# A second feed-forward product made of seven block products instead of eight, in two sweeps over its weights

## The reference, cut to what matters

```python
def hybrid_layer(x, ...):
    ...
    h = rms_norm_2(x, norm_mlp)
    return x + jnp.square(jax.nn.relu(h @ w_ff1)) @ w_ff2     # w_ff1 [1024, 4096], w_ff2 [4096, 1024]

def second_block(x, ...):
    ...
    return rms_norm_2(x, norm_final)
```

## Time and profile before

| what | value |
|---|---|
| median of three runs | 1082.27 us (1082.26 to 1082.41) |
| the profiled execution's own time | 1083.03 us |
| its span, first to last instruction | 1081.2 us |
| TensorE busy | 1060.9 us, 98% |
| VectorE / ScalarE / GpSimd busy | 555.6 / 477.5 / 125.7 us |

### The profile page before, as it was taken

One profiled execution on the slowest core, in us unless ns is written; L12 is line 12 of the kernel. 1 busy time (PEld: TensorE's weight loads), 2 busy tenths in 40 slices (PEclk: granted clock), 3 DMA queues, 4 the chain that ended last, 5 costly groups with the idle time before them and its releaser, 6 DMA issues.

```text
span 1081.2 us, 14121 instructions
## 1 busy us (share of the span) xinstructions
PE 1060.9 (98%) x5460; PEld 869.6 (80%) x5460; DVE 555.6 (51%) x1096; ACT 477.5 (44%) x893; POOL 125.7 (12%) x158
## 2 busy tenths in 40 slices
PE   9999999999899999999999999999999999999997
PEld 7788878888788888978777778898888888888885
DVE  5578997666874235434577777442222213333334
ACT  8454345555542433344677843233344433222223
POOL 0022110003400005400434400000000000000000
PEclk9999999999999999999999999999999999999999
DMA  8554333124220573132100642044222322233002
GB/s 320 113 125 99 98 93 80 43 59 158 88 88 1 157 243 115 39 81 76 40 2 1 215 156 98 1 160 171 78 78 81 140 91 78 78 96 138 1 1 79
DMA packets 74802, 104.28 MB, mean 96 GB/s; under 512 B 3904, under 2 KB 41536, under 8 KB 74736
## 3 DMA queue, kind: packets, MB, share of 16 engines
q1 hardware_dynamic: 73808, 100.60, 28.8%
q0 software_dynamic: 784, 2.75, 1.7%
q10 hardware_dynamic: 144, 0.03, 0.0%
HBM read 98.52 MB, written 4.85 MB: 96 GB/s over the span
## 4 chain that ended last, share of the span: by engine, by line
PE 84%; DVE 8%; ACT 3%; DMA 3%; issue 1%; SPq 1%; POOL 0%; DVEq 0%; ACTq 0%
PE bank L759 70%; PE bank L916 3%; PE bank L1092 2%; PE bank L897 2%; PE bank L906 2%; DVE x L1778 1%; PE bank L1014 1%; DVE stats L1777 1%; DMA arena<-in_x 1%; PE bank L1101 1%; DMA wring<-in_w_in 1%; PE bank L1115 1%; DVE u_lo L1682 1%; PE bank L807 1%; DVE x L2147 0%
## 5 line engine op out<-in xcount | busy, mean ns | idle before, releaser
L2119 DVE TENSOR_TENSOR w_lo<-wring,w_hi 128x1024 fp32r<-128x1024 f32 x64 | 78.4, 1225 | 238.1 <-ACT w_hi L1597 238.1
L1597 ACT ACTIVATE w_hi<-wring 128x1024 fp32r<-128x1024 f32 x64 | 67.7, 1058 | 211.4 <-PE bank L759 211.4
L759 PE MATMUL bank<-u_hi,h_hi 128*128 128x512 f32 (+1 forms) x288 | 111.0, 385 | 1.5 <-ACT arena L1240 1.0
L759 PE MATMUL bank<-u_hi,h_lo 128*128 128x512 f32 (+1 forms) x288 | 109.1, 379 | 0.0
L759 PE MATMUL bank<-u_lo,h_hi 128*128 128x512 f32 (+1 forms) x288 | 109.0, 379 | 0.0
L1682 DVE TENSOR_TENSOR u_lo<-wring,u_hi 128x1024 fp32r<-128x1024 f32 (+1 forms) x64 | 78.9, 1241 | 53.5 <-ACT u_hi L1332 53.0
L759 PE MATMUL bank<-h_hi,w_lo 128*128 128x512 f32 (+2 forms) x272 | 104.5, 384 | 0.0
L1332 ACT ACTIVATE u_hi<-wring 128x1024 fp32r<-128x1024 f32 (+1 forms) x64 | 65.9, 1034 | 87.3 <-PE bank L759 62.8
L759 PE MATMUL bank<-h_hi,w_hi 128*128 128x512 f32 (+2 forms) x272 | 104.4, 384 | 0.0
L759 PE MATMUL bank<-h_lo,w_hi 128*128 128x512 f32 (+2 forms) x272 | 104.3, 384 | 0.0
L759 PE MATMUL bank<-w_lo,ff_hi 128*128 128x512 f32 x256 | 101.1, 395 | 0.0
(11 more groups left out here) (296 smaller groups left out, 2065.3 us busy)
## 6 DMA issues: line engine op xcount, KB each, us to landing
wring<-in_w_ff SPq DMA_DIRECT2D x16, 2048.0 KB, 8.1
wring<-in_w_in SPq DMA_DIRECT2D x60, 512.0 KB, 3.9
arena<-in_w_out SPq DMA_DIRECT2D x4, 1024.0 KB, 5.0
wring<-in_w_out SPq DMA_DIRECT2D x2, 2048.0 KB, 12.6
arena<-in_first SPq DMA_DIRECT2D x8, 418.0 KB, 6.1
arena<-in_x SPq DMA_DIRECT2D x4, 512.0 KB, 10.7
arena<-bias_copies POOLq DMA_DIRECT2D x8, 256.0 KB, 6.4
arena<-bias_copies SPq DMA_DIRECT2D x32, 64.0 KB, 2.2
```

Of the source, the lines that this page charges most:

```text
L759: last = mm(b, lhs, rhs, start=(start and n == 0), stop=(stop and n == 2))
L1597: run(dst, src, ACT.Copy).then_inc(w_hi_done, 1)
L2119: v.tensor_tensor(cut(w_lo[ring3(m)]), src, cut(w_hi[ring3(m)]).bitcast(F32), ALU.subtract).then_inc(w_lo_done, 1)
```

## The change

The hidden channels are taken in 16 pairs of 128-channel chunks, a and b. The tokens are cut into two halves of 256, the output columns into two halves of 512. With two chunks, two token halves and two output halves a pair has eight block products; here seven are made, of sums and differences of blocks, and added into the output blocks with signs. In a first sweep over all pairs four products are made (24 matmuls of the same shape per pair: 4 products by 2 token tiles by 3), in a second sweep three (18 matmuls per pair). So 16 x 42 = 672 matmuls stand where 768 did. `w_ff2` is read from HBM twice, a pair (1 MB) at a time, into six places.

The block sums are made in place by GpSimd: `side_totals` on `ffT` (two of 128x256 per pair, while the first product runs), `side_sum` (128x256 per pair of the first sweep), `weight_sums` (one of 128x1024 and one of 128x512 per pair in the first sweep, two of 128x512 in the second). VectorE makes one further difference (`side_diff_done`, 512 columns) per pair of the first sweep. Highs and lows are made for whole pairs: the weights' 2048 columns in the first sweep and 1536 in the second, the tokens' side 256 + 768 and 256 + 512. The rings for the highs are four pairs deep (`place_free`, on `pair_used`).

Between the sweeps the last two pairs of the first are run bank by bank, and VectorE adds eight banks into `x` in twelve adds; the last four pairs (`held`) of the second sweep are also run bank by bank. The final norm's order is rewritten; for two of the four token tiles ScalarE scales and GpSimd multiplies by the gain.

The core of the diff:

```diff
+PAIR = 2 * D
+PAIR_PLACES = 6
+NP = NF // 2
+HELD = 4
 ...
@@ sync
+            for m in range(2 * NP):
+                if m < PAIR_PLACES:
+                    sp.wait_ge(w_lo_done, 4 * (6 + m // 2))
+                else:
+                    sp.wait_ge(pair_used, m - PAIR_PLACES + 1)
+                rows = w["w_ff2_2"][2 * P * (m % NP):2 * P * (m % NP + 1), :]
+                sp.dma_start(pair_raw(m).rearrange("p (k n) -> p k n", k=2), rows.rearrange("(k p) n -> p k n", p=P))\
+                    .then_inc(piece_in[pair_place(m)], 16)
@@ tensor
-            for k in range(NF - 2):
 ...
+            def product(m, t, b, tokens, cols, start, stop, low=0):
+                w = (s_hi[m % 4], s_lo[pair_place(m)])
+                f = (f_hi[m % 4], f_lo[m % 4])
+                token = slice(tokens + t * P, tokens + (t + 1) * P)
+                high, lows = slice(cols, cols + S), slice(low + cols, low + cols + S)
+                mm(b, f[0][:, token], w[0][:, high], start=start, stop=False)
+                mm(b, f[1][:, token], w[0][:, high], start=False, stop=False)
+                return mm(b, f[0][:, token], w[1][:, lows], start=False, stop=stop)
+            for m in range(NP - 2):
+                pe.wait_ge(f_lo_done, m + 1)
+                for q in range(4):
 ...
+                    for t in range(2):
+                        last = first_of(m, q, t)
+                last.then_inc(pair_used, 1)
+            for q in range(4):
+                for t in range(2):
+                    for m in (NP - 2, NP - 1):
+                        pe.wait_ge(f_lo_done, m + 1)
+                        last = first_of(m, q, t)
 ...
+            for m in range(NP, 2 * NP - HELD):
+                pe.wait_ge(f_lo_done, m + 1)
+                for q in range(3):
+                    for t in range(2):
 ...
+                        last = second_of(m, q, t)
@@ scalar
+            def place_free(m, side):
+                if m >= 4:
+                    act.wait_ge(pair_used, m - 3)
 ...
+            def pair_high(m):
+                place_free(m, "w")
+                act.wait_ge(w_summed, 2 * m + 2)
+                at = 0 if m < NP else S
+                run(s_hi[m % 4][:, 0:PAIR - at], pair_raw(m)[:, at:PAIR], ACT.Copy).then_inc(s_hi_done, 1)
@@ vector
+            def lows(m):
+                f, hi, lo, total = ff_pair(m % NP), f_hi[m % 4], f_lo[m % 4], f_sum[m % 4]
+                if m < NP:
+                    dve.wait_ge(side_sum_done, m + 1)
+                    by = total[:, 256:512].unsqueeze(1).to_broadcast([P, 2, 256])
+                    v.tensor_tensor(total[:, 512:D].rearrange("p (q s) -> p q s", q=2), f[:, 256:768].rearrange("p (q s) -> p q s", q=2),
+                                    by, ALU.subtract).then_inc(side_diff_done, 1)
+                at = 0 if m < NP else S
+                dve.wait_ge(s_hi_done, m + 1)
+                v.tensor_tensor(s_lo[pair_place(m)][:, at:PAIR], pair_raw(m)[:, at:PAIR], s_hi[m % 4][:, 0:PAIR - at].bitcast(F32), ALU.subtract)
+                dve.wait_ge(f_hi_done, m + 1)
 ...
+            for m in range(NP + 2):
+                lows(m)
 ...
+            for m in range(NP + 2, 2 * NP):
+                lows(m)
@@ gpsimd
+            def side_totals(j):
+                pool.wait_ge(a_free, AT[("ff", 2 * j + 1)] + 1)
+                f = ff_pair(j)
+                g.tensor_tensor(f[:, 256:512], f[:, 256:512], f[:, 768:D], ALU.add)
+                g.tensor_tensor(f[:, 512:768], f[:, 512:768], f[:, 0:256], ALU.add)
+            def side_sum(m):
+                if m >= 4:
+                    pool.wait_ge(pair_used, m - 3)
 ...
+                g.tensor_tensor(f_sum[m % 4][:, 256:512], f[:, 0:256], f[:, 768:D], ALU.add).then_inc(side_sum_done, 1)
+            def weight_sums(m):
+                pool.wait_ge(piece_in[pair_place(m)], 16 * (m // PAIR_PLACES + 2))
+                raw = pair_raw(m).rearrange("p (q n) -> p q n", q=4)
+                if m < NP:
+                    g.tensor_tensor(raw[:, 1:3, :], raw[:, 1:3, :], raw[:, 0:4:3, :], ALU.add).then_inc(w_summed, 1)
+                    pool.wait_ge(w_summed, 2 * m + 1)
+                    g.tensor_tensor(raw[:, 3, :], raw[:, 3, :], raw[:, 0, :], ALU.add).then_inc(w_summed, 1)
+                else:
+                    g.tensor_tensor(raw[:, 1, :], raw[:, 1, :], raw[:, 3, :], ALU.subtract).then_inc(w_summed, 1)
+                    g.tensor_tensor(raw[:, 2, :], raw[:, 2, :], raw[:, 0, :], ALU.subtract).then_inc(w_summed, 1)
+            for j in range(NP - 1):
+                side_totals(j)
 ...
+            weight_sums(2)
+            side_totals(NP - 1)
+            side_sum(1)
+            weight_sums(3)
+            side_sum(2)
+            for m in range(4, 2 * NP):
+                weight_sums(m)
+                if m <= NP:
+                    side_sum(m - 1)
```

More of the change, by code:

```diff
@@ L1171, in _ @@
             R += 2 * NT
-            NF = DFF // P
             def ff_tile(c, first, end):
@@ new lines, in _ @@
+            held = range(2 * NP - HELD, 2 * NP)
+            for m in held[:-1]:
+                pe.wait_ge(f_lo_done, m + 1)
+                for t in range(2):
+                    second_of(m, 0, t)
+            pe.wait_ge(f_lo_done, 2 * NP)
+            for t in range(2):
+                second_of(2 * NP - 1, 0, t).then_inc(p_full, 1)
+            for q in (1, 2):
+                for t in range(2):
+                    for m in held:
+                        last = second_of(m, q, t)
+                    last.then_inc(p_full, 1)
@@ L1625, in _ @@
[L1625 to L1632, removed]
+                if c == NF - 3:
+                    pair_high(0)
+                    side_high(0)
@@ new lines, in _, with square @@
+                if c == NF - 2:
+                    pair_high(1)
+            side_high(1)
+            for m in range(2, 2 * NP):
+                pair_high(m)
+                side_high(m)
+            def square(order, i, n, seen):
+                act.wait_ge(added, seen)
+                if order >= 2:
+                    act.wait_ge(ss_done, 3 * NT + order - 1)
+                run(junk[:, 512 * (order % 2):512 * (order % 2 + 1)], x[:, i, 512 * n:512 * (n + 1)], ACT.Square, accum_out=ssf[:, 2 * i + n:2 * i + n + 1])\
+                    .then_inc(ss_done, 1)
@@ L2149, in _ @@
-            dve.wait_ge(gfin_in, 16)
[L2150 to L2156, removed]
-                        finish(i - 1)
-                    if n == 0:
-                        dve.wait_ge(ss_done, 3 * NT + 2 * i + 1)
-                        v.tensor_scalar(first_half[:, i:i + 1], ssf[:, 2 * i:2 * i + 1], 1.0 / D, EPS, ALU.mult, ALU.add).then_inc(half_done, 1)
@@ new lines, in finish @@
+            def finish(n, i):
+                dve.wait_ge(inverse_done, n + 1)
+                for c in (slice(0, 512), slice(512, D)):
+                    v.scalar_tensor_tensor(x[:, i, c], x[:, i, c], rsf[:, i:i + 1], gfin[:, c], ALU.mult, ALU.mult).then_inc(y_done, 1)
+            for m in range(NP + 2):
+                lows(m)
+            for t in range(2):
+                dve.wait_ge(p_full, 1 + t)
+                add(2 + t, t, 0, ALU.add)
+                add(2 + t, 2 + t, 1, ALU.add)
@@ new lines, in _ @@
+            for t in range(2):
+                dve.wait_ge(p_full, 3 + t)
+                add(4 + t, 2 + t, 1, ALU.subtract, 2 * t + 2)
+                add(4 + t, 2 + t, 0, ALU.add)
+            for t in range(2):
+                dve.wait_ge(p_full, 5 + t)
+                add(6 + t, 2 + t, 1, ALU.add, 2 * t + 5)
+            for t in range(2):
+                dve.wait_ge(p_full, 7 + t)
+                add(t, t, 0, ALU.add, 2 * t + 1)
+            for m in range(NP + 2, 2 * NP):
+                lows(m)
@@ new lines, in _ @@
+            dve.wait_ge(gfin_in, 16)
+            for t in range(2):
+                dve.wait_ge(p_full, 9 + t)
+                add(2 + t, 2 + t, 1, ALU.add, 9 + t)
+                add(2 + t, t, 1, ALU.add)
+            half_of(2, 1, 1)
+            half_of(3, 1, 2)
+            dve.wait_ge(p_full, 11)
+            add(4, 2, 0, ALU.add, 6)
+            add(4, 0, 0, ALU.add, 11)
+            invert(0, 2)
+            finish(0, 2)
+            dve.wait_ge(p_full, 12)
+            add(5, 3, 0, ALU.add, 8)
```

200 lines of the change are left out of this document (126 added, 74 removed).

## The result

Three executions of the changed kernel took 1111.04, 1114.19 and 1115.25 us against 1082.26 us before: the ratio is 1.0289, 95% interval 1.0264 to 1.0315, slower. (A fourth execution took 5842 us; it is left out of the ratio, and nothing here explains it.) The profiled execution took 1115.25 us, its span is 1113.4 us, 32.2 more than before.

The account below looks back on a forecast made before the run. The matmul count bounds the second product before; after, alternating VectorE and GpSimd turns do. Steps reach E + 210.1 against E + 178.0, so +32.1 us with an unchanged tail: span 1113.3, time 1114 us, range 1095 to 1137.

Parts of the forecast that it names:

- What is removed: Second product: 768 - 672 = 96 matmuls at 0.2316 us go, 22.2 us, the whole gain if other engines keep pace.
- Rival (a): Second product: VectorE and GpSimd overlap after all, leaving stalls of 2.4 and 0.4 us; 1063 us, faster; chance 0.07.
- The exclusion: VectorE operations with two SBUF inputs and GpSimd operations reading SBUF alternate: 7.81 us per first-sweep pair, 4.75 per second-sweep pair.
- The sum: Five steps from the first product's end to the last matmul, plus the tail: +32.1 us, span 1113.3 us.
- E: End of the first product, 895.3 us in the trace before; the forecast's steps count from it.
- The first stall: TensorE's first wait, at pair 1, which comes at about E + 14: about 8 us standing still.
- the 9.1 us for work ahead: First sweep: GpSimd's sums of pairs 16 to 19, run ahead before pair 15's lows, 4 x 2.28 us.
- step 3: Between sweeps: TensorE runs pairs 14 and 15 bank by bank, 11.1 us; VectorE's adds keep up; pair 18's lows start at E + 134.6.
- the tail: Behind the last matmul, final adds, norm and output: about 7.9 us, no change (1 us either way).
- The overlap of 0.13 us per turn: Only an operation's fixed front overlaps the other engine's; if nothing overlaps, 23 us more, 1137 us.
- Rival (b): TensorE's clock falls to 1.2 GHz in pauses, 24 matmuls taking up to 11.1 us; part gives 1125 to 1160; chance 0.06.
- Rival (c): Alternation real but cheap, both engines at lower bounds and GpSimd's lead falling free: 1085 to 1095 us; chance 0.05.

## Why the prediction was right, point by point

- **What is removed.** 96 matmuls, 22.2 us by the prediction. The run with sums of 8 columns shows it by itself: 1062.77 us, 20.3 less than the profiled 1083.03, with 1.7 us of waiting. Rival (a) gave 1063 for a kernel without the exclusion. Of its two small stalls the one at pair 1 was there (2.3 us in the run that only writes, 2.4 forecast); the one of 0.4 us at pair 31 shows in neither run.
- **The exclusion.** Forecast from two stretches of the trace before, where the same kinds of operation met by chance. (One reading there was off by an instruction: the MAX8 of rows 8 had ended at 156.60 us, and what ran beside GpSimd's add of 1.04 us was MATCH_REPLACE8, 0.67 us from 156.72 on. No subtract with two SBUF inputs was beside it until 157.43, 0.2 us before its end, so the argument stands.) Shown by four runs: it goes when GpSimd only writes, shrinks with the number of reading sums, appears in the kernel before when reading adds are put beside it, and is absent where VectorE's second input is in PSUM. Rival (a) has fallen.
- **The sum.** E was 894.9. VectorE began pair 1 at 898.6, E + 3.7 (forecast 3.6). The first stall was 8.0 us (8). The lows of pair 15 ended at 1015.4, E + 120.6 (122.6): GpSimd was not as far ahead as assumed. It began its sums for pair 19 at 1014.5, so part of the 9.1 us for work ahead lay behind this point instead. The prediction thought such sums free there, in the seam. They weren't: the lows of pairs 16 and 17 took 7.4 us instead of the 5.2 that they take in a later run without sums beside them, and VectorE's adds followed with no gap:

```profile
1022.75 7.25 DVE L2254 TENSOR_TENSOR x<-x,bank 128x512 f32<-128x512 f32 x12
```

So VectorE set the length of the seam, not TensorE's 48 matmuls as step 3 has it, and the lows of pair 18 began at 1029.9, 14.5 us behind pair 15 and not 12: E + 135.0 (134.6). In the second sweep VectorE stood still for 4.0 us, not 1, for pair 20, whose transfer came late; GpSimd's sums ran by themselves meanwhile, and from pair 18 to the end of pair 31's lows it took 63.4 us (63.0). The lows of pair 31 ended at 1093.3, E + 198.5 (197.6); the last matmul at 1106.2, E + 211.4 (210.1); the tail took 7.2 us (7.9). Span 32.2 us longer (32.1). The terms erred by up to 3 us, in both directions, and cancelled: the mechanism and the size of the turns were right, but the agreement of the span within 0.1 us is luck.
- **The overlap of 0.13 us per turn**, against the letter of the exclusive lock, held for the whole instruction, of the Trainium skill ("SBUF — State Buffer", section "SBUF: two separate sides"), held: 2.15 of 2.29 us and 0.58 of 0.73 in the turns shown, 0.14 and 0.15 us. With nothing overlapping it would have been 23 us more (the prediction's estimate). What that page of the Trainium skill says in the same section on which operations exclude each other, two SBUF inputs on the one side and a GpSimd operation that reads SBUF on the other, agrees with the runs: VectorE ran free beside the memsets, and GpSimd beside the adds from PSUM.
- **Rival (b), the clock.** It did fall in the pause at pair 1 and in short stretches later, and cost nothing that the sum needs: VectorE had no idle time between pair 1 and the end of the seam, its lows set the pace, and TensorE still waited for them in 12 of 15 pairs. The matmuls at the lower level (0.43 us apart, from 908.65 to 912.65) only made its next wait shorter. Where TensorE sets the pace the clock does count, as the run that only writes shows.
- **Rival (c)**, cheap turns, fell too: the turns had the sizes of the sum, and GpSimd's lead was not free.

What went wrong was in the expectations for the versions with VectorE's sums: four of them ended 2 to 5 us above the range. A pair of the first sweep took 6.40 us where 6.2 were reckoned (pair to pair in the run with the sums ahead); waits of VectorE for its own semaphore were left out, which may be the difference, though the run that took one of them away gained only 0.9 us, within its spread. The start was misjudged twice: once the sums ran past the end of the first product, once ScalarE's queue held the relu behind them.

## What to carry to other kernels

A spare engine is only spare if it may run beside the busy one. Before moving elementwise work to GpSimd, look in the trace for a place where its reading operations meet VectorE's operations with two SBUF inputs; if the durations stretch there, add the two engines' times instead of taking the larger. Here a pair's sums cost VectorE 4.0 us in the first sweep when GpSimd made them (the prediction's term, which the turns bear out) and 2.4 us when VectorE did (1.87 for the weights' sums and 0.52 for the side sum, start to start, in the run with the sums ahead); in the second sweep 2.3 and 1.2 us. The place where GpSimd's sums cost nothing was beside VectorE's reads of PSUM.

A high busy share is not yet work. VectorE was busy for 20.00 of 20.00 us here while its instructions took on average up to three times what the same shapes take elsewhere. The list of waits didn't show that; the mean durations by shape did.

## What the hardware showed that was not expected

- A GpSimd sum of 8 columns beside VectorE's subtracts takes 0.76 us on average in the run with one sum left out, from 0.27 to 2.14 us, though almost nothing is computed: a small operation waits, too, and sometimes nearly the whole of a 2048-column subtract. Whether splitting GpSimd's sums into small operations would help was not tried.
- GpSimd's memsets of 1024 columns, 0.957 us, over tensors that VectorE reads with two inputs, lengthened none of its operations (2.285 us for 2048 columns).
